# Reordering two instruction lists of a fused transformer block, and copying only two of three plain weight quarters into PSUM

## The reference, cut to what matters

```
def _ffn_sublayer(x, shift, scale, gate, pre_g, post_g, w_gu, w_down):
    h = _modulate(_rmsnorm(x, pre_g), shift, scale)
    a, b = jnp.split(h @ w_gu, 2, axis=-1)
    y = (jax.nn.silu(a) * b) @ w_down
    return x + FFN_RES_WEIGHT * gate * _rmsnorm(y, post_g)

    x = _ffn_sublayer(x, ...ffn1...);  cx = _ffn_sublayer(cx, ...ffn1...)
    h = _modulate(_rmsnorm(x, mix_pre), mod[3], mod[4]);  hc = the same of cx
    y = _mixer(h, hc, w_in, ...)          # delta rule and attention, a merge, an output projection
    x = x + mod[5] * _rmsnorm(y, mix_post)
    x = _ffn_sublayer(x, ...ffn2...)      # x alone; only x is returned
```

## Time and profile before

| | |
|---|---|
| median of three runs | 1915.96 us |
| the profiled execution | 1915.56 us, span 1913.9 us |
| PE busy | 1861.7 us (97%) |
| DVE, ACT, POOL busy | 1259.0, 976.4, 526.5 us |
| mixer norm and its join to the next block | 577 to 605 us |
| start of the second FFN | 1560 to 1590 us |
| its three chunks of products | 1573 to 1631, 1675 to 1760, 1803 to 1865 us |

### The profile page before, as it was taken

The page is one execution under the profiler, slowest core; times in us unless marked ns, Lnnn a source line. Parts: engine busy times, 40 slices in busy tenths (PEclk is TensorE's granted clock), DMA queues, the critical chain, the costliest instruction groups (busy, mean ns, idle before and its releaser), DMA issues.

```text
span 1913.9 us, 32275 instructions
## 1 busy us (share of the span) xinstructions
PE 1861.7 (97%) x11917; PEld 1739.8 (91%) x11917; DVE 1259.0 (66%) x2099; ACT 976.4 (51%) x1869; POOL 526.5 (28%) x398
## 2 busy tenths in 40 slices
PE   8899999999998999999999999999999989999997
PEld 5899999999997799999999999997888979899897
DVE  7758787878666765467666766676333577376476
ACT  6534242424447655557555755574223566375463
POOL 0714141323100300255345534550000034142330
PEclk9999999999999999999999999999999999999999
DMA  8133335553423410011111111111333403223232
GB/s 334 60 122 124 129 110 164 173 189 122 137 77 118 120 61 1 23 40 61 49 33 38 60 49 33 38 45 56 99 99 112 141 23 112 87 89 121 78 133 67
DMA packets 52241, 178.36 MB, mean 93 GB/s; under 512 B 6820, under 2 KB 10020, under 8 KB 51888
## 3 DMA queue, kind: packets, MB, share of 16 engines
q1 hardware_dynamic: 48864, 162.46, 25.1%
q0 software_dynamic: 3280, 14.60, 2.4%
HBM read 170.17 MB, written 4.24 MB: 91 GB/s over the span
## 4 chain that ended last, share of the span: by engine, by line
PE 75%; DVE 9%; ACT 7%; issue 5%; POOL 2%; DMA 2%; SPq 0%; ACTq 0%; DVEq 0%; POOLq 0%
PE ps L2603 51%; PE ps L2814 14%; PE ps L2607 4%; PE ps L2901 2%; DMA raw<-W 2%; PE ps L3135 1%; PE ps L3059 1%; DVE e_lo L2007 1%; ACT e_hi L1253 1%; DVE d_os L2497 1%; ACT ps L1238 1%; DVE d_c L2365 1%; PE ps L3089 1%; PE ps L3191 1%; ACT w_hi L929 1%
## 5 line engine op out<-in xcount | busy, mean ns | idle before, releaser
L2603 PE MATMUL ps<-h_hi,w_hi 128*128 128x512 f32 (+2 forms) x736 | 245.2, 372 | 9.4 <-DVE h_lo L1788 3.0
L2603 PE MATMUL ps<-h_lo,w_hi 128*128 128x512 f32 (+2 forms) x736 | 241.2, 360 | 0.0
L2603 PE MATMUL ps<-h_hi,w_lo 128*128 128x512 f32 (+2 forms) x736 | 232.2, 356 | 0.0
L1718 DVE TENSOR_TENSOR w_lo<-raw,w_hi 128x1024 fp32r<-128x1024 f32 (+1 forms) x99 | 123.6, 1248 | 132.5 <-ACT w_hi L929 132.5
L929 ACT ACTIVATE w_hi<-raw 128x1024 fp32r<-128x1024 f32 (+1 forms) x99 | 103.8, 1048 | 157.6 <-PE ps L2603 155.7
L2603 PEld LDWEIGHTS ps<-h_hi,w_hi 128*128 128x128 f32 x736 | 132.8, 188 | 29.9 <-DVE h_lo L1788 6.6
L2603 PEld LDWEIGHTS ps<-h_hi,w_lo 128*128 128x128 f32 x736 | 136.0, 188 | 13.4
L2603 PEld LDWEIGHTS ps<-h_lo,w_hi 128*128 128x128 f32 x736 | 136.0, 188 | 12.9 <-issue 1.2
L2603 PE MATMUL ps<-g_hi,w_hi 128*128 128x384 f32 (+2 forms) x444 | 132.9, 346 | 0.8 <-DVE w_lo L1718 0.5
L2603 PE MATMUL ps<-g_hi,w_lo 128*128 128x384 f32 (+2 forms) x444 | 131.8, 343 | 0.0
L2603 PE MATMUL ps<-g_lo,w_hi 128*128 128x384 f32 (+2 forms) x444 | 131.8, 343 | 0.0
(11 more groups left out here) (457 smaller groups left out, 5440.7 us busy)
## 6 DMA issues: line engine op xcount, KB each, us to landing
raw<-W SPq DMA_DIRECT2D x221, 512.0 KB, 3.5
w_mod<-WMOD SPq DMA_DIRECT2D x68, 512.0 KB, 3.9
g_row<-g_rows POOLq DMA_DIRECT2D x8, 768.0 KB, 4.5
X<-XT SPq DMA_DIRECT2D x4, 768.0 KB, 6.8
a_sw<-i_n POOLq DMA_DIRECT2D x40, 64.0 KB, 1.9
w_first<-WMOD SPq DMA_DIRECT2D x4, 512.0 KB, 10.9
X<-XT SPq DMA_DIRECT2D x1, 2048.0 KB, 13.2
x_spill<-X POOLq DMA_DIRECT2D x1, 2048.0 KB, 8.5
```

What stands on the lines that cost most here:

```text
L1718: v.tensor_tensor(lo, src, hi.bitcast(F32), ALU.subtract).then_inc(s("w_split"), 1)
L2603: return pe.matmul(out, lhsT, rhs, start=start, stop=stop)
```

## The change

In words:

- **Mixer norm:** behind each second add (and square) of part 2 stands one tile of part 1, so four tiles of part 1 are done among the adds; PE's sums of part 2 stand between the slices of part 1. Block `B_QKV + 2` gets weights of its own place, and they are split before part 2's tiles on ACT and behind them on DVE.
- **Copies:** A22 is not copied to PSUM; its remainder is taken from `raw`, in SBUF.
- **Start of the second FFN:** blocks 4 and 5 wait for the readers of blocks 0 and 1 (whose bank they take) and no longer for those of blocks 2 and 3. On DVE `first_gate(5)` and `token_lo2(2)` move ahead of the remainders of S1 and A22.
- **Chunk borders:** the first six quarters of a chunk are prepared in steps j = 4, 5, 6.
- **Last down projection:** its third block is split ahead of the loop, on ACT ahead of a table load.

```diff
         def weights(b):
+            if isinstance(b.n, int) and b.n == B_QKV + 2:
+                return q2_hi[:], q2_lo[:]
...
         def copy_bank(pos):
-            return ps[:, 5 + (A11, A12, A22).index(pos), :].rearrange("p (k n) -> p k n", k=4)
+            return ps[:, 5 + (A11, A12).index(pos), :].rearrange("p (k n) -> p k n", k=4)
...  ACT, ffn1_last
                 for k in range(KT):
                     ffn1_x_square(2, k)
-                for k in range(KT):
+                    if k % 2:
+                        mix_tile(1, k // 2)
+                for k in range(4, KT):
                     mix_tile(1, k)
-                    if k == 3:
+                    if k == 5:
                         ffn1_rstd("x", 2)
+                a.wait_ge(s("gemm_done"), B_QKV)
+                split(Blk(B_QKV, 0, 2))
                 for k in range(KT):
                     mix_tile(2, k)
...  ACT, last_down (DVE likewise: split(blks[2]) ahead of the loop)
-                    if i + 2 < KT:
+                    if 0 < i < KT - 2:
                         split(blks[i + 2])
...  ACT, weights_hi
-                if pos in (A11, A12, A22):
+                if pos in (A11, A12):
                     copy_weights(q, pos)
+                if pos == A22:
+                    blk = pair_blocks(q)[1]
+                    a.wait_ge(w_loaded[blk.raw], (blk.load + 1) * 16)
...  ACT, ffn2
                     if c == 2:
+                        split(Blk(B_LAST, 0, 2))
                         a.preload_act_table_set(LOG_SET)
...  ACT and DVE, ffn2
-                        for p in PLAN2[c + 1][0][0][2 * j - 10:2 * j - 8] if j >= 5 else ():
+                        for p in PLAN2[c + 1][0][0][2 * j - 8:2 * j - 6] if j >= 4 else ():
...  ACT, after the mixer norm (DVE likewise: no step at m = 0)
-                step(Blk(B_QKV, 0, m))
+                if m:
+                    step(Blk(B_QKV, 0, m))
+                else:
+                    a.wait_ge(s("gemm_done"), B_QKV + 1)
...  DVE, ffn1_last
                 for k in range(KT):
                     ffn1_add(2, k)
-                for h in (1, 2):
-                    for k in range(KT):
-                        mix_low(h, k)
+                    if k % 2:
+                        mix_low(1, k // 2)
+                for k in range(4, KT):
+                    mix_low(1, k)
+                for k in range(KT):
+                    mix_low(2, k)
+                split(Blk(B_QKV, 0, 2))
...  DVE, weights_lo
-                src = copy_bank(pos) if pos in (A11, A12, A22) else weight_part2(q, pos)
+                src = copy_bank(pos) if pos in (A11, A12) else weight_part2(q, pos)
...  DVE, ffn2
                 token_lo2(0)
+                first_gate(5)
+                token_lo2(2)
                 weights_lo(0, S1)
                 weights_lo(0, A22)
-                token_lo2(2)
-                first_gate(5)
                 token_lo2(3)
...  PE, ffn1_last
-                for k in range(KT):
-                    ffn1_x_sum(2, k)
                 for h in (1, 2):
                     for k in range(KT + 1):
+                        for m in (2 * k, 2 * k + 1) if h == 1 and k < 4 else ():
+                            ffn1_x_sum(2, m)
...  PE, ffn2, blocks 4 and 5
-                pe.wait_ge(psum_read[blk.pair], blk.turn + 1)
+                    pe.wait_ge(psum_read[blk.pair], blk.ahead(-4).turn + 2)
```

More of the change, by code:

```diff
@@ L315, in build @@
         c_u = at("c_u", 205, [2, CTX])
+        q2_hi = at("q2_hi", 132, [KT, P], F32R)
+        q2_lo = at("q2_lo", 136, [KT, P], F32R)
         tail_w = [at(f"tail_w{i}", 142 + 24 * i, [2, FCH[2], P], F32R) for i in range(2)]
@@ L1230, in copy_weights @@
             def copy_weights(q, pos):
-                blk = pair_blocks(q)[int(pos == A22)]
+                blk = pair_blocks(q)[0]
                 a.wait_ge(w_loaded[blk.raw], (blk.load + 1) * 16)
@@ L1870, in last_down @@
                 v.memset(y_acc[:, CTX:T], 0.0).then_inc(s("ysq_used"), 1)
+                split(blks[2])
                 for i, blk in enumerate(blks):
@@ L2906, in ffn2 @@
                 first_up()
-                gemm(Blk(B_FFN2, 0, 4), f_hi, f_lo, segs_x, off=CTX)
-                blk = Blk(B_FFN2, 0, 5)
-                pe.wait_ge(s("w_split"), blk.w + 1)
-                pe.wait_ge(psum_read[blk.pair], blk.turn + 1)
[L2911 to L2916, removed]
+                for blk in (Blk(B_FFN2, 0, 4), Blk(B_FFN2, 0, 5)):
+                    pe.wait_ge(s("w_split"), blk.w + 1)
+                    pe.wait_ge(psum_read[blk.pair], blk.ahead(-4).turn + 2)
+                    for k in range(KT):
+                        for i, (w, x) in enumerate(((w_hi, f_hi), (w_hi, f_lo), (w_lo, f_hi))):
+                            last = mm(bank(blk, 1), w[:, blk.pair, k, :], x[:, k], k == 0 and i == 0, k == KT - 1 and i == 2)
+                        if k == 3 and blk.j == 5:
+                            last.then_inc(s("d_mm"), 1)
+                    last.then_inc(s("gemm_done"), 1)
                 for c in range(3):
```

## The result

The changed kernel takes 1920.33 us (median of 10 runs, 1919.09 to 1921.38) where the kernel before takes 1915.26 us (10 runs beside it): the medians differ by +5.07 us. The ratio of the runs is 1.0023 with a 95% interval of 1.0014 to 1.0031, which is +4.4 us, between +2.7 and +5.9. The forecast was 1921.0. The profiled execution has a span of 1918.8 us (before 1913.9).

A forecast was written before the change was run, and what follows sets the result against it. It took a ring of ACT and DVE, not PE, to bound the chunks. Norm +1.5, chunk 0 -0.5, chunk 1 +2.5, chunk 2 +2.4 and last projection -0.9 sum to +5.0: 1921.0 us, 8-in-10 range 1913.6 to 1925.5.

The forecast's parts named there:

- the ring: Second FFN chunks: a cycle of waits between ACT and DVE, not PE, sets the lap of 10.46 us.
- A22 from `raw`: Chunk laps: the remainder waits for POOL's running sum in 13 of 19 pairs; chunk 1 +2.5, chunk 2 +2.4 us.
- Rival 1: Chunk laps: A22's remainder does not wait for POOL; total -2.1, 1913.9 us; chance 0.15.
- rival 2: Chunk laps: each contended A22 remainder pays the full 1.1 us; about +12, 1928 us; chance 0.12.
- The norm: Mixer norm and join together: net +1.5 us, with bounds of -1.7 and +3.0.
- The stall and the join: Mixer norm: DVE waits for ACT's rounding at four tiles, last tile 604.66 not 601.70; PE starts 606.7 not 605.21.
- three rounds of 3.46: Mixer norm: each round of two adds and a tile takes 3.46 us instead of 2.65; fourth tile 2.84 late.
- The start of the second FFN: Earlier gate and no bank wait bring the second pair's `f_pa` to 1588.7 instead of 1590.01: -1.3 us.
- the old half clock at 1579: Start of the second FFN: the clock reading of 0.50 after PE's gap should not come.
- near 585 in the norm: Sign of being wrong: the clock falls among thin PE work there; one earlier half-clock stretch cost some 1.5 us.
- Chunk borders: Chunk 1: first `f_pa` 0.6 earlier, but the second waits for PE's own A12, so little is left.
- Last projection: Last down projection: earlier split leaves only the bank's read, done 1870.1, instead of a 1.03 us PE wait: -0.9.

The follow-up runs named there:

- early_both: Kernel before, with ACT's copies of A11 and A12 moved ahead of its waits for `f_pa`'s silu and the gate: 1911.19 us, ratio 0.9976.
- best_both: Kernel before plus early A11 and A12 copies, early join, second FFN start, chunk borders and last projection; no norm interleave, A22 copied: 1905.68 us, ratio 0.9947.
- c_alone: Kernel before with only A22's remainder taken from `raw`, without the copy: 1921.44 us, ratio 1.0029.
- pool_short: Changed kernel with three quarters of POOL's S3 and S1 sums left out from the third pair on, all waits kept: 1914.62 us.
- c_undone: Changed kernel with A22 copied to PSUM again, all other parts kept: 1914.04 us, ratio 0.9991.
- start_alone: Kernel before with only the new start of the second FFN, A22 still copied: 1914.19 us, ratio 0.9994.
- after_early: Changed kernel with ACT's copies of A11 and A12 moved ahead of its waits: 1911.75 us, ratio 0.9982.
- norm_alone: Kernel before with only the mixer norm's interleaved lists, third block's weights split at the old place: 1917.08 us, ratio 1.0008.
- early_a11: Kernel before with only ACT's copy of A11 moved ahead of its wait for `f_pa`'s silu: 1912.04 us, ratio 0.9985.
- join_alone: Kernel before with the third block's weights in their own place and split around part 2's tiles, no interleave: 1913.97 us, ratio 0.9993.

## Why the prediction was right, point by point

- **What bounds the chunks.** Shown: taking two copies of ACT out of the ring, with no work less, makes five of ten inner laps 10.06 to 10.09 instead of 10.46 in early_both, and 9.99 to 10.08 in best_both; adding to DVE's part of the ring makes them 10.9 to 11.5. PE's 49.98 busy of 50 was no sign of a bound PE. One reading in the prediction is off: it has twelve more distances like 10.46 in chunks 1 and 2, but only eight of the twelve there are inner laps, seven of 10.46 to 10.49 and one of 10.74. Nothing in its sum rests on that.
- **A22 from `raw`.** Shown, with its size. The 13 laps named are the 13 that pay. The forecast took what was left of POOL's instruction in the old trace; c_alone, where nothing else moves, gives +1.65, +2.54 and +2.28 where the rows gave 1.5, 3.1 and 1.9 for it. So the single phases were less well known than their sum. In the changed kernel the 13 exceed 0.69 by 8.96 together, where the old trace's phases gave 9.19 - 13 x 0.13 = 7.5: the loads and POOL's sums do not stand where they stood. Rival 1 (no wait) would need remainders of 0.69; rival 2 (full price) needs 1.79 each; the largest is 1.74 and the mean 1.38.
- **The norm: the term that was mis-sized,** +0.92 where I had +1.5. The stall and the join came as told (DVE's wait is 1.09 in three rounds and 0.78 in the first; PE 2.17 behind the last tile's start, forecast 2.0). But I counted three rounds of 3.46, and they are 3.43, 3.43 and 2.98. The last is short: there is no next add whose scaling (0.34) has to be done, and the two adds run back to back. That is 0.5 of the 0.6 missed.
- **The start of the second FFN.** PE's A12 at 1574.94 (forecast 1574.7), `f_pa` at 1581.47 (1581.3), and PE's wait of 1.82 for L1308 (1.9 for L1297 of before): nearly as told. For the second pair I had 1588.7; it came at 1589.07, from a remainder of 1.50 where I had 1.4, and 0.2 by which the whole profile was later. From gate to chunk 0's end the term was -0.5 and the profile shows +0.33, since the waits of 1.50, 1.52 and 1.58 exceed the forecast (1.39, 1.14, 1.38) by about 0.7 together. That the start itself gives about 2 us while the clock stays up shows in pool_short, where these waits are gone: chunk 0 is 2.2 shorter, and rival 1 had 2.0.
- **The chance in it.** That number rests on the clock staying up. Here it did. In c_undone and start_alone, with the same 1.82 us of idle, it fell and took back about 1.3. The prediction said of the old half clock at 1579 only that it should not come, and gave no chance to one behind the new wait; that the clock stayed up in the profile of the changed kernel is luck of that size. The fall that its last paragraph does name, near 585 in the norm, came in c_undone and cost nothing. There (first line) and in the changed kernel (second line) PE starts the same nine matmuls, and the norm takes 41.59 and 41.60:

```profile
585.00:588.00 3.00, 2.82 (x9) 1.64 (x9) 1.92 (x6) 1.61 (x4) 0.00 (x0) 0.51 0.01 3
585.00:588.00 3.00, 1.95 (x9) 0.94 (x8) 1.92 (x6) 1.72 (x4) 0.00 (x0) 1.00 0.01 3
```

- **Chunk borders.** No gain or loss of its own shows: with A22 copied, chunks 1 and 2 of c_undone are as before to 0.04. The first `f_pa` of chunk 1 comes 0.6 earlier there (4.60 behind the chunk's first product, before 5.21) and the second does not (11.71 and 11.73), as told. This part was not tried by itself.
- **Last projection.** -0.83 for -0.9.

By stage the errors are -0.6 (norm), +0.8 (chunk 0), +0.3, +0.1 and +0.1, together +0.7, and the medians differ by +5.07 for a forecast of +5.0. That agreement is closer than the terms are, and closer than the interval can tell: the errors of -0.6 and +0.8 cancel for the most part, and in the profile 0.75 us of lead from before the first mark offsets what is left.

## What to carry to other kernels

Moving an operand from PSUM to SBUF can cost time although a copy disappears: ask which other engine is at work at that instant, and whether the copy stood in the ring that sets the pace. Where busy shares say "bound by PE", compare the distance of equal instructions from lap to lap with PE's own need (here 10.46 and 10.08); a difference points to a ring. A copy that fits into an idle gap ahead of its engine's wait may be moved there, but only if the engines fed by loads still keep their distance. And test a bundle of edits by stage: here the parts that read `raw` and interleave the norm lost 6.4 and 2.3 us and hid that the others gained.

## What the runs showed of the hardware that was not expected

The granted clock behind a short gap of PE does not follow from the code at that place. After 1.82 to 1.84 us of idle at the new start of the second FFN it stayed at 1.00 in the profiles of the changed kernel, pool_short, best_both and after_early, and fell to 0.50 for about 3 us in those of c_undone and start_alone. After 3.3 us of idle at the old start it fell in before, c_alone, early_both, norm_alone and early_a11, and stayed up in join_alone (1.00 in each window from 1575 to 1585). After 1.70 us at the join it fell in start_alone and not in the five other profiles with that wait. Near 90 us, behind 2.2 us of idle, it fell in eight of the twelve profiles and not in four; three of the four (join_alone, start_alone, early_a11) are 1.9 to 2.0 us ahead of before at the norm's first mark, the fourth (after_early) 1.0.

What a fall costs depends on where it comes: 1.2 to 1.6 us at the start of the second FFN and at the join (join_alone and before differ by 1.2 in chunk 0, the norms of start_alone and before by 1.6), and nothing in c_undone's norm, where PE was waiting for DVE anyway. join_alone's profiled run, with none of these falls, is at 1911.04 where its median is 1913.97. (Every profile, this one too, has one more fall 5 to 9 us before its end.) I take this to be a part of the scatter between runs (join_alone: 1910.88 to 1915.97). The timed runs bear that out as far as they can: each has its mean granted clock beside its time, and over the 110 runs of the eleven changed kernels, each taken against its own kernel's mean, lower clock goes with longer time (correlation -0.62, about four tenths of the variance). It was not tried by itself.
